# A two-block transformer step in one kernel: VectorE instead of GpSimd sums the rows of w_ada, one fused multiply-add per 128x1024 piece

## The chip, the core and the metric

One Trainium2 chip, of which the kernel uses one core. The metric is the time of the whole program on the device in microseconds, the median of several runs. The profile comes from one execution of its own, taken by the hardware profiler.

## What is computed

A batch of one sequence, 256 tokens of 2048 features in float32, goes through a first block and then a second one. Cut to what matters here:

```
c_act = silu(c)                                  # (1, 2048)
mod   = c_act @ w_ada + b_ada                    # w_ada: 2048 x 12288
sh1, sc1, gt1, sh2, sc2, gt2 = split(mod, 6)     # 6 pieces of 2048

h = rms_norm(x, g_mix) * (1 + sc1) + sh1
z = h @ w_in                                     # q, k, v (two attentions), indexer, gates
merged = sigmoid(gate_sb) * (stick_breaking(z) @ w_o_sb) + sigmoid(gate_ds) * (top64_attention(z) @ w_o_dsa)
x = x + gt1 * (merged @ w_out)

h = rms_norm(x, g_ffn) * (1 + sc2) + sh2
x = x + gt2 * ((silu(conv3(h @ w_gate)) * (h @ w_up)) @ w_down)
x = rms_norm(x, g_final)
# second block: gated linear attention, then a SwiGLU of the same width (5632)
```

The product `c_act @ w_ada` has a single row on the left. It isn't made by matmuls with w_ada as an operand: for each group of 128 rows of w_ada, all its rows are scaled by their entry of c_act, and the 16 groups are added up in one tile of 128 partitions; TensorE then adds the 128 partitions with a vector of ones.

## The kernel before, in words

**Matmuls.** Every large product is made in float32 accuracy from rounded parts. A weight slab of 128x2048 numbers (1 MB, four blocks of 128 rows by 512 columns) is fetched into `raw`, a ring of 4 slabs. A half is half a slab, 128x1024. ScalarE casts each half into `whi` (line 818), VectorE subtracts to get the remainder `wlo` (line 1206, "the split"), and TensorE makes 12 matmuls of 512 columns per half (lines 391 to 393). `whi` and `wlo` are rings of 4 halves, so a cast of half i waits until TensorE is through with half i-4, and at most three finished halves lie ahead of TensorE.

**Stages.** The list PHASES names them: A (48 halves, q, k, v of the first attention; an 80-column projection of the indexer lies between halves 15 and 16), B (64 halves, with the stick-breaking attention between them, one head per 8 halves), C1 (32, with the indexer's scores), C2 (32, it begins with a top-64 on VectorE and has the sparse attention between halves), O (32, output projections), U (32, w_out), F1p, F1 and F1e (16, 240 and 8 halves, the feed-forward), then the second block: GQ, GV, GR, GO, F2p, F2, F2e. With 24, 32, 16, 16, 16, 16 and 8 slabs, the stages A to F1p hold slabs 0 to 127. `body` on ScalarE and VectorE runs 4 halves ahead of its stage: its index idx goes from 4 to 19, and steps of attention, drains of PSUM and so on are hooks that run behind the split of a given idx. All engines work their programs in order.

**w_ada.** Pieces 0 and 1 (sh1, sc1) are summed at the very start by VectorE, in one `scalar_tensor_tensor` per 128x4096 rows (line 1273). The other four (4, 3, 2, 5 in that order: sc2, sh2, gt1, gt2) are summed by GpSimd in the background of A to F1: a chunk of 128x1024 (512 KB) comes into one of the two buffers of `ada_in`, GpSimd multiplies it by a column of c_act that it has copied into `acol` (line 1766), in place (line 1758), adds it to `ada_acc` (line 1760), and counts it in `ada_left`. There are 32 chunks per piece, 128 in all. When a piece is complete, TensorE adds the partitions: `ada_columns(0)` and `ada_columns(1)` (line 435, sc2 and sh2 as columns) behind A and behind C1, `ada_rows` (line 442) in U and in F1e. GpSimd clears `ada_acc` in between (line 1774). GpSimd also lays out the heads for the attentions (`sb_stage`, `ix_stage`, `qk_stage`, `v_stage`), between two pairs of chunks.

**The order of the fetches.** SyncE issues all DMAs, in program order. A slab waits until the slab four before it has been split (`lo_made`, line 233), a chunk until the chunk two before it has been added (`ada_left`, line 240). The chunks stand between slabs. Behind A, SyncE writes the table of distance biases to DRAM, waits for it, and loads 16 shifted copies of it into `hank0` and `hank1` (lines 285 to 293), which C2 uses.

Of the kernel before, what the change touches and what calls it, by code (L numbers as in the profile page):

```python
# [5 lines left out]
P = 128  # L6
S = 256
TB = S // P
D = 2048
KT = D // P  # L10
NB = 512
# [39 lines left out]


def build_program(nc, A, out):
# [28 lines left out]
    ada_in = at("ada_in", [P, 2, D // 2], ADA)  # L82
    ada_acc = at("ada_acc", [P, D], ADA + 8 * KB)
# [139 lines left out]
    ada_left = sem("ada_left")  # L223
# [5 lines left out]
    def _(sp):  # L229
        def slab(it, phase, per, s, src):  # L230

            if not (phase == "A" and s < RING and isinstance(it, int)):
# [3 lines left out]
        def ada_chunk(n, piece, j):  # L236

            if not (isinstance(n, int) and n < 2):
                sp.wait_ge(ada_left, n - 1)
            kt, half = (j // 2, j % 2) if isinstance(j, int) else j  # L240
# [26 lines left out]
        def a_body(it):  # L267
            for s in range(8):
                slab(it, "A", 16, s, w_in[:, 4 * (s % 4):4 * (s % 4) + 4, ds(it * 2 * NB + s // 4 * NB, NB)])
                ada_chunk(8 * it + s + 8, 4, ((8 * it + s + 8) // 2 if isinstance(it, int) else 4 * it + s // 2 + 4, s % 2))  # L270
        for s in range(RING):
            slab(0, "A", 16, s, w_in[:, 4 * s:4 * s + 4, 0:NB])
        for j in range(6):
            ada_chunk(j, 4, j)
        for s in range(RING, 8):
            slab(0, "A", 16, s, w_in[:, 4 * (s % 4):4 * (s % 4) + 4, NB:2 * NB])
            for j in range(2):
                ada_chunk(6 + 2 * (s - RING) + j, 4, 6 + 2 * (s - RING) + j)
        for j in range(14, 16):
            ada_chunk(j, 4, j)  # L280
        with sp.Fori(1, 3) as it:
            a_body(it)
# [3 lines left out]
        sp.wait_ge(sem("e_out"), 16)  # L286

        sp.wait_ge(sem("tt_T"), KT // 2)
        for h in range(NH):
            src = e_dram[h:h + 1, 0:P]  # L290
            sp.dma_start(hank1[:, h, :], bass.AP(tensor=src.tensor, offset=src.offset, ap=[[1, P], [1, S]])).then_inc(sem("hank_in"), 16)
            src = e_dram[h:h + 1, P:2 * P]
# [1711 lines left out]
```

## Time and profile before

| | |
|---|---|
| median of 3 runs | 3091.49 us (3090.83 to 3091.84) |
| profiled execution, first to last instruction (its span) | 3088.4 us |
| what lies around the span, against the median | 3.1 us |
| TensorE busy | 2772.0 us, 90% |
| VectorE busy | 2006.4 us, 65% |
| ScalarE busy | 1288.5 us, 42% |
| GpSimd busy | 1037.5 us, 34% |
| mean granted TensorE clock | 0.960 |
| moved by DMA | 585.40 MB, mean 190 GB/s |

The profiled execution has no time of its own beside its span. In the profile, PE is TensorE, PEld its weight load, DVE is VectorE, ACT ScalarE, POOL GpSimd, and SP SyncE. "Clock" is the share of the full clock that the throttle granted to TensorE; there are two levels, 0.5 and 1. A busy share is a mean over the span, and the stages of this kernel differ; so the rows below cut the span at the ends of the stages. "x" counts instructions that begin in a stretch. An L with a number is a line of the program before.

### The profile page before, as it was taken

The page shows a single profiled execution, that of the slowest core. Times are in us where ns is not written, and L with a number is a line of the kernel's source. Part 1 is how long each engine was busy: PE and PEld are TensorE (multiplying, and loading weights), DVE is VectorE, ACT ScalarE, POOL GpSimd, SP SyncE. Part 2 cuts the span into 40 slices and gives each one's busy share as a digit, 9 for nine tenths or more (in the row PEclk, how much of TensorE's full clock was granted, in tenths as well). Part 3 has the DMA queues.
Part 4 walks back from the last instruction along what each step waited for, and adds up shares of the span by engine and source line. Part 5 has one row for each costly group of instructions (what it writes and reads, how often), then busy time and mean ns, then how long its engine had stood idle before and what let it go on. Part 6 is the DMA issues. An engine that isn't in the chain of part 4 may idle for free. (4 is left out here: it accounts for less than half of the span.)

```text
span 3088.4 us, 35464 instructions
## 1 busy us (share of the span) xinstructions
PE 2772.0 (90%) x12279; PEld 2258.1 (73%) x12279; DVE 2006.4 (65%) x1808; ACT 1288.5 (42%) x1505; POOL 1037.5 (34%) x538
## 2 busy tenths in 40 slices
PE   0599899989988799999999959998898999999998
PEld 0477787667767678888788748777587888888886
DVE  7776566887975777677766674456655555555554
ACT  1223455334433444444444434444245444444443
POOL 0598454858945433222322250002200111111111
PEclk9989899989999899999999979998999999999999
DMA  9666554746664665655666515454054555555553
GB/s 392 240 205 230 198 206 175 245 144 210 242 234 164 236 204 190 204 195 191 198 204 207 187 55 187 153 177 150 1 164 152 190 190 190 190 191 190 189 190 122
DMA packets 266919, 585.40 MB, mean 190 GB/s; under 512 B 14300, under 2 KB 16676, under 8 KB 263900
## 3 DMA queue, kind: packets, MB, share of 16 engines
q1 hardware_dynamic: 266844, 584.41, 56.1%
q8 instruction: 45, 0.74, 0.1%
q14 instruction: 30, 0.25, 0.0%
HBM read 582.26 MB, written 2.11 MB: 189 GB/s over the span
## 5 line engine op out<-in xcount | busy, mean ns | idle before, releaser
L1206 DVE TENSOR_TENSOR sb_wlo<-sb_raw,sb_whi 128x1024 fp32r<-128x1024 f32 x896 | 1322.9, 1487 | 883.4 <-ACT sb_whi L818 882.5
L818 ACT ACTIVATE sb_whi<-sb_raw 128x1024 fp32r<-128x1024 f32 x896 | 945.2, 1059 | 1452.8 <-PE lin L393 1250.8
L391 PE MATMUL lin<-sb_whi,sb_act_hi 128*128 128x512 f32 x2880 | 1154.9, 401 | 89.7 <-DVE sb_wlo L1206 46.4
L393 PE MATMUL lin<-sb_whi,sb_act_lo 128*128 128x512 f32 x2880 | 1136.2, 395 | 0.0
L392 PE MATMUL lin<-sb_wlo,sb_act_hi 128*128 128x512 f32 x2880 | 1136.0, 394 | 0.0
L391 PEld LDWEIGHTS lin<-sb_whi,sb_act_hi 128*128 128x128 f32 x2880 | 550.7, 191 | 218.9 <-issue 53.2
L393 PEld LDWEIGHTS lin<-sb_whi,sb_act_lo 128*128 128x128 f32 x2880 | 549.6, 191 | 117.9
L392 PEld LDWEIGHTS lin<-sb_wlo,sb_act_hi 128*128 128x128 f32 x2880 | 551.3, 191 | 111.8 <-issue 0.2
L1758 POOL TENSOR_TENSOR sb_ada_in<-sb_ada_in,sb_small 128x1024 f32<-128x1024 f32 x128 | 301.0, 2351 | 293.5 <-DMA sb_ada_in<-in_w_ada_dram 174.7
L1760 POOL TENSOR_TENSOR sb_ada_acc<-sb_ada_acc,sb_ada_in 128x1024 f32<-128x1024 f32 x128 | 383.4, 2995 | 10.0
L391 PE MATMUL lin<-sb_whi,sb_hid_hi 128*128 128x512 f32 x704 | 278.4, 395 | 6.3 <-DVE sb_hid_lo L1487 3.7
L392 PE MATMUL lin<-sb_wlo,sb_hid_hi 128*128 128x512 f32 x704 | 275.5, 391 | 0.0
L393 PE MATMUL lin<-sb_whi,sb_hid_lo 128*128 128x512 f32 x704 | 275.5, 391 | 0.0
L1891 POOL TENSOR_TENSOR sb_x<-sb_x,sb_dstage 128x512 f32<-128x512 f32 x44 | 76.9, 1749 | 398.1 <-ACT sb_dstage L832 398.1
L1891 POOL TENSOR_TENSOR sb_yacc<-sb_yacc,sb_dstage 128x512 f32<-128x512 f32 x44 | 83.5, 1899 | 368.1 <-ACT sb_dstage L832 368.1
L391 PEld LDWEIGHTS lin<-sb_whi,sb_hid_hi 128*128 128x128 f32 x704 | 133.2, 189 | 37.6 <-DVE sb_hid_lo L1487 4.1
L393 PEld LDWEIGHTS lin<-sb_whi,sb_hid_lo 128*128 128x128 f32 x704 | 133.1, 189 | 28.1
L392 PEld LDWEIGHTS lin<-sb_wlo,sb_hid_hi 128*128 128x128 f32 x704 | 133.2, 189 | 27.3 <-issue 0.2
L1942 POOL TENSOR_TENSOR sb_ge<-sb_gb 128x256 f32<-128x256 f32 x24 | 17.5, 731 | 314.7 <-PE lin L393 282.9
L1897 POOL TENSOR_TENSOR sb_ubuf<-sb_ubuf,sb_cacc 128x512 f32<-128x512 f32 x11 | 19.5, 1773 | 257.5 <-ACT sb_ubuf L832 257.5
L453 PE MATMUL aux<-sb_onehot,sb_relb 32*8 32x512 f32 x2 | 1.9, 1036 | 87.8 <-DMA sb_relb<-in_rel_bias_dram 87.8
L1273 DVE SCALAR_TENSOR_TENSOR sb_acc<-sb_ada,sb_small,sb_acc 128x4096 f32<-128x4096 f32 x16 | 71.7, 4483 | 4.7 <-DMA sb_ada<-in_w_ada_dram 4.1
(292 smaller groups left out, 1770.5 us busy)
## 6 DMA issues: line engine op xcount, KB each, us to landing
sb_raw<-in_w_in_dram SPq DMA_DIRECT2D x88, 1024.0 KB, 5.9
sb_raw<-in_ffn_w_gu_dram SPq DMA_DIRECT2D x88, 1024.0 KB, 5.1
sb_ada_in<-in_w_ada_dram SPq DMA_DIRECT2D x128, 512.0 KB, 3.9
sb_raw<-in_gla_w_in_dram SPq DMA_DIRECT2D x48, 1024.0 KB, 5.2
sb_raw<-in_w_gate_dram SPq DMA_DIRECT2D x44, 1024.0 KB, 5.3
sb_raw<-in_w_up_dram SPq DMA_DIRECT2D x44, 1024.0 KB, 5.2
sb_raw<-in_w_down_dram SPq DMA_DIRECT2D x44, 1024.0 KB, 5.1
sb_raw<-in_ffn_w_down_dram SPq DMA_DIRECT2D x44, 1024.0 KB, 5.0
```

The source lines that it names most:

```text
L391: pe.matmul(o, x_hi[:, kt + q, t], whi[:, w], start=first and q == 0, stop=False)
L392: pe.matmul(o, x_hi[:, kt + q, t], wlo[:, w], start=False, stop=False)
L393: m = pe.matmul(o, x_lo[:, kt + q, t], whi[:, w], start=False, stop=last and q == 1)
L453: pe.matmul(aux[3][0:NH, :], relb[:], onehot[:], start=True, stop=True).then_inc(sem("erow_T"), 1)
L818: act.activation(whi[:, idx % RING * HALF:(idx % RING + 1) * HALF], raw[:, idx // 2 % RING, idx % 2 * HALF:(idx % 2 + 1) * HALF], ACT.Copy ...
L1206: dve.tensor_tensor(wlo[:, c], raw[:, idx // 2 % RING, idx % 2 * HALF:(idx % 2 + 1) * HALF], whi[:, c].bitcast(fp32), ALU.subtract).then_i ...
L1273: dve.scalar_tensor_tensor(acc0[:], ada0[:, u, :], cact[:, ds(4 * it + u, 1)], acc0[:], ALU.mult, ALU.add).then_inc(sem("ada0_sum"), 1)
L1758: pool.tensor_tensor(ada_in[:, half, :], ada_in[:, half, :], col.to_broadcast([P, D // 2]), ALU.mult).then_inc(sem("ada_mul"), 1)
L1760: pool.tensor_tensor(ada_acc[:, c], ada_acc[:, c], ada_in[:, half, :], ALU.add).then_inc(sem("ada_sum"), 1)
L1891: pool.tensor_tensor(y[:, 0, s], y[:, 0, s], dstage[:, c % 2, :], ALU.add).then_inc(sem("dstage_free"), 1)
L1897: pool.tensor_tensor(ubuf[:, 0, :], ubuf[:, 0, :], cacc[:].rearrange("p a t -> p (a t)")[:, 0:NB], ALU.mult).then_inc(sem("up_mul"), 1)
L1942: pool.tensor_tensor(e[:, :, 1, :], b[:, :, 1, :], ref, ALU.subtract)
```

## The change

VectorE takes over the 128 chunks. Each is one instruction: the chunk times an entry per partition of c_act, plus the sum so far. The first chunk of each half of a piece is a plain multiplication that overwrites, so nothing is cleared. The first piece has a tile of its own, `ada_first`, in the space of x, whose content is used up by then. GpSimd keeps only its other work, and its layouts no longer stand between pairs of chunks.

The chunks are dealt to slabs by a table, CHUNKS_AT: chunk n belongs to slab n+4 (n under 64), n+8 (under 96), n+20 (under 102); 102 and 103 belong to slabs 124 and 125, 104 and 105 to slab 126, 106 and 107 to slab 127. SyncE fetches the chunk right behind its slab, once the chunk two before it is added. VectorE adds it behind the split of the slab's second half and that half's hooks. In F1 the chunks keep their place in SyncE's order, and VectorE adds them at idx 21 and 23.

Three things move. The table loads go from behind A to behind the first slab of C1's second half. `ada_columns(0)` goes from behind A to behind B, and what VectorE makes of it (`mod_made`) with it; `ada_columns(1)` from behind C1 into C1, behind half 27. Loops of A, B, C1, C2 and O are written out where a chunk's number has to be a constant.

```
+ADA_PIECES = (4, 3, 2, 5)
+CHUNKS_AT = {}
+for _n in range(108):
+    _at = 4 + _n if _n < 64 else 8 + _n if _n < 96 else 20 + _n if _n < 102 else (124, 125, 126, 126, 127, 127)[_n - 102]
+    CHUNKS_AT.setdefault(_at, []).append(_n)
+def chunks_after(phase, it, per, s):
+    return CHUNKS_AT.get(H0[phase] // 2 + it * per // 2 + s, []) if isinstance(it, int) else []
...
+    ada_first = at("ada_first", [P, D], XB)
...
 SyncE
         def slab(it, phase, per, s, src):
...
             sp.dma_start(raw[:, s % RING, :].rearrange("p (k n) -> p k n", k=4), src).then_inc(slab_in[s % RING], 16)
+            for n in chunks_after(phase, it, per, s):
+                ada_chunk(n)
+        def ada_chunk(n, kt=None, half=None):
             if not (isinstance(n, int) and n < 2):
-                sp.wait_ge(ada_left, n - 1)
+                sp.wait_ge(sem("ada_sum"), n - 1)
...
+        for it in range(4):
+            cols_body(it, "B", 6 * NB)
+        def hankels():
+            sp.wait_ge(sem("e_out"), 16)
+            sp.wait_ge(sem("ada_T"), 1)
+            for h in range(NH):
...
+        for it in range(2):
+            cols_body(it, "C1", C_GATE, hankels if it else None)
...
 TensorE
         m.then_inc(sem("kix_T"), 1)
-        ada_columns(0)
...
-        pe.wait_ge(sem("mod_made"), 1)
...
         pe.wait_ge(sem("sb_out"), NH)
+        ada_columns(0)
...
+                if (it, idx) == (1, 11):
+                    pe.wait_ge(sem("mod_made"), 1)
+                    ada_columns(1)
...
 VectorE
+        def ada_add(n, kt=None, half=None):
+            first = isinstance(n, int) and n % 32 < 2
+            if kt is None:
+                kt, half = n % 32 // 2, n % 2
+            acc = ada_first if isinstance(n, int) and n < 32 else ada_acc
+            c = slice(half * (D // 2), (half + 1) * (D // 2))
+            dve.wait_ge(ada_come[half], 8 * (n - half) + 16)
+            if first:
+                if n >= 64:
+                    dve.wait_ge(sem("ada_T"), n // 32)
+                dve.tensor_scalar(acc[:, c], ada_in[:, half, :], cact[:, kt:kt + 1], None, ALU.mult).then_inc(sem("ada_sum"), 1)
+            else:
+                dve.wait_ge(sem("ada_sum"), n - 1)
+                dve.scalar_tensor_tensor(acc[:, c], ada_in[:, half, :], cact[:, ds(kt, 1)], acc[:, c], ALU.mult, ALU.add).then_inc(sem("ada_sum"), 1)
         def body(it, phase, per, hooks, upto=None, start=RING):
             for idx in range(start, per + RING if upto is None else upto):
                 split(it, phase, per, idx)
                 for step in hooks.get(idx, ()):
                     step()
+                if idx % 2:
+                    for n in chunks_after(phase, it, per, idx // 2):
+                        ada_add(n)
...
+                if n == 0 and phase == name:
+                    for half in range(2):
+                        add(21 + 2 * half, lambda half=half: ada_add(108 + 2 * it + half, 6 + it, half))
...
 GpSimd
-        def ada(n, kt, half, col):
-        def pairs_of(n, kt, count):
-        def clear(piece):
...
-        def b_pool(it, more):
+        with pool.Fori(0, 3) as it:
             for u in range(2):
-                kk = 2 * it + u
-                pairs_of(32 + 2 * kk, kk, 16 + kk)
-                if more:
-                    pool.wait_ge(sem("sb_o"), 2 * it + u + 1)
-                    sb_stage(2 * it + u + 2, u)
+                pool.wait_ge(sem("sb_o"), 2 * it + u + 1)
+                sb_stage(2 * it + u + 2, u)
```

## Rows read from the trace of the kernel before

**Rows 1.** The page, part 1: busy us, share of the span, instructions
```profile
PE 2772.0 (90%) x12279; PEld 2258.1 (73%) x12279; DVE 2006.4 (65%) x1808; ACT 1288.5 (42%) x1505; POOL 1037.5 (34%) x538
```

**Rows 2.** Stages; window, length, busy us per engine (instructions), clock, DMA share, GB/s
```profile
113.20:195.40 82.20, 58.45 (x226) 45.67 (x227) 76.61 (x34) 25.74 (x35) 77.68 (x36) 0.92 0.48 154
195.40:225.20 29.80, 29.80 (x146) 27.19 (x145) 17.41 (x8) 7.12 (x8) 27.34 (x14) 0.71 0.81 273
225.20:301.30 76.10, 76.10 (x336) 62.69 (x334) 56.01 (x28) 27.89 (x28) 71.05 (x29) 1.00 0.67 225
301.30:328.30 27.00, 7.36 (x36) 7.26 (x35) 7.54 (x11) 6.28 (x8) 2.98 (x4) 0.58 0.72 253
328.30:532.10 203.80, 199.90 (x909) 165.73 (x910) 126.77 (x126) 109.63 (x127) 98.68 (x47) 0.98 0.55 196
532.10:653.50 121.40, 106.30 (x472) 81.90 (x470) 102.57 (x69) 44.35 (x61) 93.93 (x52) 0.93 0.61 208
653.50:787.70 134.20, 120.47 (x566) 99.88 (x565) 103.89 (x145) 49.70 (x91) 102.91 (x56) 0.94 0.54 188
787.70:895.50 107.80, 93.39 (x388) 74.97 (x387) 104.78 (x58) 51.24 (x50) 92.49 (x37) 0.94 0.72 253
895.50:1011.30 115.80, 101.86 (x424) 82.07 (x424) 68.46 (x53) 38.16 (x42) 52.80 (x27) 0.93 0.51 175
1011.30:1081.00 69.70, 52.00 (x234) 43.15 (x234) 54.36 (x54) 36.46 (x47) 25.56 (x16) 0.88 0.66 228
...
1094.30:1767.60 673.30, 664.57 (x2984) 544.91 (x2983) 473.82 (x455) 307.98 (x337) 187.37 (x85) 1.00 0.61 199
2331.20:2389.00 57.80, 49.34 (x225) 41.25 (x226) 32.28 (x38) 32.73 (x43) 1.27 (x1) 0.91 0.44 145
```

**Rows 3.** The same for line 393 alone (4 matmuls per half), in B and C1
```profile
354.60:403.60 49.00, 25.00 (x64) 12.02 (x64) 1.00 0.59 210
...
641.30:653.50 12.20, 6.24 (x16) 3.00 (x16) 1.00 0.32 123
```

**Rows 4.** The page, part 5: GpSimd's multiplication and addition, busy us, mean ns
```profile
L1758 POOL TENSOR_TENSOR sb_ada_in<-sb_ada_in,sb_small 128x1024 f32<-128x1024 f32 x128 | 301.0, 2351 | 293.5 <-DMA sb_ada_in<-in_w_ada_dram 174.7
L1760 POOL TENSOR_TENSOR sb_ada_acc<-sb_ada_acc,sb_ada_in 128x1024 f32<-128x1024 f32 x128 | 383.4, 2995 | 10.0
```

**Rows 5.** SyncE's own waits; waiting line and releaser, total us, times, longest
```profile
SPq L241 <- POOLq L1762: 641.2, 98, 25.2
```

**Rows 6.** Line 1206 in A and in F2; count, ns minimum/median/maximum
```profile
L1206 DVE TENSOR_TENSOR sb_wlo<-sb_raw,sb_whi x48: 1210/2372/3418, 113.8 to 293.9; 128x1024 fp32r<-128x1024 f32 x48
...
L1206 DVE TENSOR_TENSOR sb_wlo<-sb_raw,sb_whi x240: 1224/1225/1227, 2390.2 to 3049.3; 128x1024 fp32r<-128x1024 f32 x120
```

**Rows 7.** Line 1206 alone by stage, A, C2 and O: length, VectorE busy us
```profile
113.80:301.30 187.50, 110.94 (x48) 0.92 0.61 202
...
653.50:787.70 134.20, 64.17 (x32) 0.94 0.54 188
787.70:895.50 107.80, 74.68 (x33) 0.94 0.72 253
```

**Rows 8.** The page, part 5: the fused operation at 128x4096
```profile
L1273 DVE SCALAR_TENSOR_TENSOR sb_acc<-sb_ada,sb_small,sb_acc 128x4096 f32<-128x4096 f32 x16 | 71.7, 4483 | 4.7 <-DMA sb_ada<-in_w_ada_dram 4.1
```

**Rows 9.** The page, part 6: slabs of w_in, KB each, median us to landing
```profile
sb_raw<-in_w_in_dram SPq DMA_DIRECT2D x88, 1024.0 KB, 5.9
```

**Rows 10.** Timeline of TensorE, the start of F2p: start, us, idle before
```profile
2339.66 3.67 PE L421 MATMUL aux<-sb_con,sb_xs 128*128 128x128 f32 x16 [8.50 <-ACT sb_xs L855]
```

**Rows 11.** Timeline of SyncE behind A: issues
```profile
289.86 0.33 SPq L241 DMA_DIRECT2D sb_ada_in<-in_w_ada_dram  x1
...
301.48 0.39 SPq L234 DMA_DIRECT2D sb_raw<-in_w_in_dram  x1
```

**Rows 12.** Timeline of VectorE in B: first hook of a head, next splits
```profile
366.69 0.54 DVE L1324 TENSOR_SCALAR sb_lb<-aux 128x384 f32<-128x384 f32 x1
...
371.91 3.49 DVE L1206 TENSOR_TENSOR sb_wlo<-sb_raw,sb_whi 128x1024 fp32r<-128x1024 f32 x3
```

More of the change, by code:

```diff
@@ L265, in _, with cols_body @@
         sp.dma_start(relb[:], A["rel_bias"]).then_inc(sem("rel_in"), 16)
-        def a_body(it):
+        def cols_body(it, phase, col0, after=None):
             for s in range(8):
[L269 to L282, printed above, removed]
+                slab(it, phase, 16, s, w_in[:, 4 * (s % 4):4 * (s % 4) + 4, it * 2 * NB + col0 + s // 4 * NB:it * 2 * NB + col0 + s // 4 * NB + NB])
@@ L284, in _ @@
+                if after and s == 0:
+                    after()
+        for it in range(3):
+            cols_body(it, "A", 0)
         sp.wait_ge(sem("erow_held"), 1)
         sp.dma_start(e_dram, erow[:]).then_inc(sem("e_out"), 16)
[L286 to L292, printed above, removed]
-            sp.dma_start(hank0[:, h, :], bass.AP(tensor=src.tensor, offset=src.offset, ap=[[1, P], [1, P]])).then_inc(sem("hank_in"), 16)
@@ L314, in _ @@
+        for it in range(2):
+            cols_body(it, "C1", C_GATE, hankels if it else None)
+        for it in range(2):
+            cols_body(it, "C2", C_GATE + D)
+        for it in range(2):
+            for s in range(8):
+                c = it * 2 * NB + s // 4 * NB
+                slab(it, "O", 16, s, w_o[s % 4 // 2][:, 4 * (s % 2):4 * (s % 2) + 4, c:c + NB])
         sp.wait_ge(half_used, H0["O"])
@@ L1300, in _ @@
         body(0, "A", 16, drains2(0, "A", lambda k: sbz[:, 1, k * NB:(k + 1) * NB], {9: [split_ix]}), start=8)
-        with dve.Fori(1, 3) as it:
+        for it in range(1, 3):
             body(it, "A", 16, drains2(it, "A", lambda k: sbz[:, 1, cols(it, k)]))
@@ L1361, in ix_dve @@
             return {4 * u + 6: [lambda u=u: add(u)] for u in range(4)}
-        with dve.Fori(0, 2) as it:
+        for it in range(2):
             body(it, "C1", 16, drains2(it, "C1", lambda k: gate_sb[:, 1, cols(it, k)], ix_dve(it)))
@@ L1405, in ds_dve @@
             return hooks
-        with dve.Fori(0, 2) as it:
+        for it in range(2):
             body(it, "C2", 16, drains2(it, "C2", lambda k: gate_ds[:, 1, cols(it, k)], ds_dve(it)))
@@ L1428, in o_hooks @@
             return {4 * gi + 7: [lambda gi=gi: take(gi)] for gi in range(4)}
-        with dve.Fori(0, 2) as it:
+        for it in range(2):
             body(it, "O", 16, o_hooks(it))
@@ L1813, in _ @@
         ix_stage(1, 1)
[L1815 to L1826 removed]
+        for p in range(2, NIX // 2):
+            pool.wait_ge(sem("ix_T"), p - 1)
+            ix_stage(p, p)
         def qk_stage(h, u):
```

121 lines of the change are left out of this document (26 added, 95 removed).

## The prediction

> **What bounds the kernel now.** The first thing to read is the share of each engine over the whole span [rows 1]: TensorE 90%, VectorE 65%, GpSimd 34%. Taken alone it says "TensorE-bound", and that would leave this change nothing to win. So the next view is the busy time by stage [rows 2], cut where TensorE ends the last matmul of a stage. From 1094 us on TensorE is busy for 664.6 of 673.3 us, and behind that come stages that the change doesn't touch. From 113 to 1094 us it isn't: TensorE works 7.4 of the 27 us behind A, and idles 10 to 25% of C1, C2, O, U and F1p, at a granted clock of 0.88 to 0.94 (1.00, that is 2.4 GHz, in the end of A, where it never pauses).
>
> The yardstick is a stretch in which TensorE never waits. A half (one 128x1024 piece, 12 matmuls) takes 76.1/28 = 2.72 us in the end of A [rows 2], 49.0/16 = 3.06 us in B, where attention matmuls lie between, and 12.2/4 = 3.05 us in the end of C1 [rows 3]. A slab (1 MB, two halves) therefore takes 5.44 us at the least.
>
> Against that stand three costs of GpSimd's sum. First, its own pace: a piece takes 2.35 + 3.00 us [rows 4], with the waits between and a column copy for every second one about 6.0 (an estimate: GpSimd is busy 71 of 76 us in the end of A for some 12 pieces, [rows 2]), over the 5.44 us of a slab. Second, the order on SyncE: the fetch of the next piece waits for GpSimd, 641 us in total over 98 waits, and the next slab stands behind it [rows 5]. Third, VectorE: a split lasts 1.225 us without variation where GpSimd is quiet, and 1.21 to 3.42 us in A [rows 6]. 3.42 is 1.2 plus about one GpSimd instruction. Times the counts: A's 48 splits take 110.9 us instead of 58.8, C2's 32 take 64.2 instead of 39.2, O's 33 take 74.7 instead of 40.4 [rows 7].
>
> The Trainium skill says the same in SBUF — State Buffer, "Who interferes with whom": a VectorE instruction with two SBUF inputs and a GpSimd instruction that reads SBUF exclude each other, and the later one is blocked until the other ends. By that rule the trace agrees (1.21 against 3.42 us). The same skill has a rule that speaks against this change, in Perfetto Trace Analysis, "Optimizing Scalar/DVE Operations": with a saturated VectorE, handing work to ScalarE or even GpSimd may pay; it adds that between VectorE and GpSimd this may fail because of the shared port. Followed to its end it gives the second rival below.
>
> **What the change adds.** 108 pieces outside F1's loop and 20 in it move to VectorE, one instruction each. The trace has the same operation at 128x4096: 4483 ns [rows 8], a quarter of which is 1.12 us; the split, also two SBUF inputs of 1024, takes 1.225 [rows 6]. I take 1.23; 1.12 and, if something else still holds it up, 1.6 are the ends. In all 128 x 1.23 = 157 us of VectorE, against 301 + 383 = 684 us of GpSimd removed [rows 4]. Per slab of A that is 2 x 1.225 + 1.23 = 3.7 us plus 0.3 for a drain, under 5.44: hidden. On SyncE a piece now waits until the piece two before it is added, that is until VectorE is past slab s-2, so slab s+1 starts three slabs ahead and no longer four. That leaves about 5 halves x 2.72 minus 3.5 us (cast, split, add) = 10 us for a landing of 5.9 us [rows 9]: hidden too, with 4 us to spare.
>
> **Stage by stage, all against the profiled execution** (span 3088.4 us; the timed runs have a median of 3091.5, 3.1 us around the span):
> - Head of A. TensorE starts at 113.2 and is through 16 halves at 195.4. The same work stands undisturbed in F2p: first transposes at 2339.7, 16 halves done at 2389.0, 49.3 us [rows 10]. A must split four halves first, 3.4 us more. So 53 instead of 82: -29. The other 105.9 us of A (the 80-column projection at a clock of 0.71, then full pace) stay.
> - A to B. The 27.0 us before B and the first half-clock halves go. SyncE issued a piece at 289.9 and the next slab only at 301.5 [rows 11]; between them stand 16 loads of the distance table and one round trip, and these move into C1. The 32 column sums, nearly all of the 7.4 us that TensorE works there [rows 2], move behind B. What stays: split 19, drain, one add of 1.23 ahead of kdup, two copies, transposes, a cast: about 6.3 us, 0.7 of transposes and 3 at the lower clock. B's 64 halves at 3.06 are 196.2. 206.2 against 230.8: -25. B is the tightest: per 8 halves VectorE has 8 x 1.225 + 4 x 1.23 + about 7.9 us (the 5.2 us from 366.7 to 371.9 of a head's first hook, 1.7 of its second, a drain; [rows 12]) = 22.6 of 24.5 us.
> - C1. 32 halves at 3.12 us (12.2 per four where no drain falls in [rows 3], 12.5 taken) = 99.8, column sums twice (3.7 each at full clock, an estimate: half of 6.8 us at the lower one, and a little), 1.2 of start, 2 at the lower clock, 1.5 for the 16 table loads that now lie in SyncE's queue ahead of a slab (7.5 us of issue, 4 of them covered by the lead in fetches, the rest by 6 us of prepared halves). 112 against 121.4: -9. Bounds of the table loads: 0 and 6.
> - C2. It begins with 15 us of top-k on VectorE, which stays and gets one add ahead of it. After that splits save 64.2 - 39.2 = 25 us and 16 adds put back 20. TensorE idles 13.7 us here [rows 2], most of it in the top-k and where a head's softmax meets splits, and both stay: -2, from -7 to +8.
> - O. Per four halves 4.9 + 2.5 + 2.0 = 9.4 of 10.9 us: full pace, 7 x 10.9 = 76.2, and 20 for the first four, with a wait of 6 us for the splits of attention's output. 96.4 against 107.8: -11.
> - U. TensorE idles 13.9 of 115.8 us [rows 2], 5 of them at the start; the other 9, and 4 for halves at the lower clock after them, are slabs that stood on SyncE behind a piece waiting for GpSimd; the row sum and the start stay: -13.
> - F1p. 57.8 us of F2p [rows 2] is the undisturbed case, plus 2 for a table load and gate transposes: 60 against 69.7: -10.
> - Into F1: pieces 104 to 107 come two at a time behind slabs 126 and 127, and behind them on SyncE the four loads of biases and gains, then F1's first slab. That slab is now asked for once half 9 of F1p is split, then only behind the add at half 13: 4 x 2.72 = 11 us later, with 6 to 9 us of cover (the lead in fetches and three prepared halves): +4, from 0 to 10.
> - F1 and what follows: two adds at idx 21 and 23, where VectorE idles 1.5 us per half; the stage is at TensorE's pace: 0, from -9 (its small waits go) to +5.
>
> Sum: -29 - 25 - 9 - 2 - 11 - 13 - 10 + 4 = -95. 3091.5 - 95 = 2996 us (span 2993).
>
> **The rivals.**
> 1. VectorE becomes the bound (the rule on saturated engines, as a mechanism here). In B it has 1.9 us to spare per head, and its hooks wait in order for ScalarE's exponentials. One add falls between the two hooks of a head and delays the second by 1.2 us. If an add costs 1.6 us or a cast comes late, each of 8 heads loses 2 us, C1 wins 3 instead of 9, C2 loses 8 instead of winning 2: +16, +6 and +10, so 3028. For it: 92% load. Against it: TensorE has up to three prepared halves, 9 us, to live on, and a head's burst, 5.2 + 1.2 + 1.7 us, is shorter.
> 2. Slabs come late, because each stands behind an add. If landing with a piece in front is 1 to 2 us longer than the spare, 104 slabs lose 0.6 us each: +62, so 3058. Against it: the end of A already fetches nearly the same bytes per slab at 225 GB/s with the engines of the queues busy 0.67 of the time [rows 2].
> 3. Slower than before: the same loop, binding hard. Three slabs may be under way per landing L plus 4.7 us of cast, splits and add, so a slab costs (L + 4.7)/3. It binds from L = 11.6 us. To eat all that is won from 225 us to 1011 us, each of the 110 slabs there would have to cost what it does now, 786/110 = 7.1, and with the 29 us of A's head 7.4: L = 17.5 us, against a median of 5.9 [rows 9]. Were L 19, a slab would cost 7.9 and the time would be about 3091.5 + 0.5 x 110 = 3146.
> 4. More is given back than I count: C2 keeps all 7, F1's waits go, nothing is lost into F1: 2996 - 5 - 9 - 4 = 2978.
>
> **How the numbers follow.** Forecast 0.58, 2996, with its own range 2975 to 3015; rival 1 0.20, rival 2 0.07, rival 3 0.03, rival 4 0.10, and 0.02 for no change, by two of them together. The range reaches up to rival 1 with its upper terms and down below rival 4: 2962 to 3045. Faster by over 0.2% 0.95, within 0.2% 0.02, slower by over 0.2% 0.03; 0.2%, 6 us, is about what a measurement of this kernel can tell from no change.
>
> **What would show each step.** Splits at 1.225 us nearly all through; about 50 us for the first 16 halves; under 12 us between A's last matmul and B's first; 12.2 us per four halves in B; no ScalarE cast waiting for a slab DMA in U; the stretch behind 1094 us as long as now. The forecast is wrong if TensorE waits for the weights in B (rival 1), if casts wait for slab DMAs in every stage (rivals 2 and 3), or if the new instruction takes much over 1.25 us.

## The result

| | before | changed |
|---|---|---|
| median | 3091.4 us (4 runs) | 2989.2 us (4 runs, 2983.2 to 2992.8) |
| profiled execution, span | 3088.4 us | 2990.8 us (its own time 2992.77 us) |
| ratio of the times | | 0.967, 95% interval 0.9657 to 0.9684 |

The change is 102 us faster, 3.3%. Forecast were 2996 us, from 2962 to 3045. Between the two profiled spans lie 97.6 us; all shares below are parts of these. First the page of the changed kernel, part 1 (as [rows 1]): busy us, share of the span, instructions.

```profile
PE 2749.4 (92%) x12279; PEld 2248.6 (75%) x12279; DVE 1850.3 (62%) x1936; ACT 1291.7 (43%) x1505; POOL 303.6 (10%) x214
```

VectorE has 128 instructions more than before and 156 us less busy time, though the adds are in it (128 x 1.28 = 164 us, by the row below). So its other instructions got 320 us shorter together: what GpSimd's work had put on them [rows 6]. The next line is of the changed kernel's page, part 5: the fused add. Below it stands the split (before L1206, now L1205) in A alone (count, ns minimum/median/maximum).

```profile
L1222 DVE SCALAR_TENSOR_TENSOR sb_ada_acc<-sb_ada_in,sb_small,sb_ada_acc 128x1024 f32<-128x1024 f32 x90 | 114.9, 1279 | 0.0
```

```profile
L1205 DVE TENSOR_TENSOR sb_wlo<-sb_raw,sb_whi x51: 1217/1226/1228, 113.1 to 270.7; 128x1024 fp32r<-128x1024 f32 x51
```

In A the split has no variation left (before 1210 to 3418 ns). The add takes 1.28 us; 1.23 was forecast. Now the stages of the changed kernel, cut as [rows 2] at TensorE's last matmul of each: window, length, busy us of PE, PEld, DVE, ACT and POOL, clock, DMA share, GB/s. In order they are the head of A (16 halves), the rest of A, A's end to B's end, C1, C2, O, U, F1p, the first four halves of F1, and the rest of F1.

```profile
112.52:166.37 53.85, 50.94 (x227) 42.27 (x227) 38.21 (x42) 28.46 (x37) 0.00 (x0) 0.97 0.57 198
166.37:272.30 105.93, 105.91 (x480) 89.91 (x479) 60.45 (x52) 35.94 (x36) 0.00 (x0) 0.92 0.69 238
272.30:477.00 204.70, 198.14 (x911) 164.76 (x912) 150.17 (x164) 112.35 (x132) 7.46 (x8) 0.98 0.70 245
477.00:590.10 113.10, 112.28 (x532) 89.61 (x531) 69.00 (x84) 44.28 (x61) 12.15 (x12) 0.94 0.66 226
590.10:713.20 123.10, 112.74 (x534) 93.99 (x534) 91.61 (x161) 50.61 (x91) 6.26 (x12) 0.96 0.58 203
713.20:808.40 95.20, 90.28 (x389) 74.12 (x387) 71.44 (x71) 50.03 (x50) 0.00 (x0) 0.96 0.76 270
808.40:911.00 102.60, 96.67 (x424) 78.94 (x424) 64.29 (x61) 40.58 (x45) 9.88 (x6) 0.97 0.61 211
911.00:971.40 60.40, 50.49 (x233) 41.82 (x232) 42.32 (x50) 30.81 (x41) 4.67 (x3) 0.92 0.52 173
971.40:992.20 20.80, 14.65 (x58) 11.95 (x58) 14.03 (x18) 10.96 (x11) 0.00 (x0) 0.84 1.03 383
992.20:1665.30 673.10, 664.22 (x2984) 545.43 (x2983) 446.50 (x473) 307.94 (x334) 75.86 (x40) 1.00 0.60 198
```

Against [rows 2], in us:

| stage | before | changed | difference | forecast |
|---|---|---|---|---|
| A, to its end | 188.1 | 159.8 | -28.3 | -29 |
| A's end to B's end | 230.8 | 204.7 | -26.1 | -25 |
| C1 | 121.4 | 113.1 | -8.3 | -9 |
| C2 | 134.2 | 123.1 | -11.1 | -2 |
| O | 107.8 | 95.2 | -12.6 | -11 |
| U | 115.8 | 102.6 | -13.2 | -13 |
| F1p | 69.7 | 60.4 | -9.3 | -10 |
| first four halves of F1 | 13.3 | 20.8 | +7.5 | +4 |
| rest of F1 | 673.3 | 673.1 | -0.2 | 0 |
| behind F1 | | | +4.6 | 0 |

(0.7 us are missing in the table: TensorE starts A that much earlier. "Behind F1" reaches to the end of the span.) Most of the gain came where it was forecast. Three lines are off: C2 won five times as much, F1 begins later than expected, and 4.6 us are lost behind F1, where no instruction was changed.

### The profile page after: what moved, and what is told of

It is laid out like the page before. It is cut to its first block and busy times, and to the rows that moved or that the text cites. A ratio compares the mean times of both kernels' runs of the same rounds, so it can differ in the third digit from the quotient of the medians.

```text
span 2990.8 us, 34105 instructions
## 1 busy us (share of the span) xinstructions
PE 2749.4 (92%) x12279; PEld 2248.6 (75%) x12279; DVE 1850.3 (62%) x1936; ACT 1291.7 (43%) x1505; POOL 303.6 (10%) x214
## 5 line engine op out<-in xcount | busy, mean ns | idle before, releaser
L1205 DVE TENSOR_TENSOR sb_wlo<-sb_raw,sb_whi 128x1024 fp32r<-128x1024 f32 x896 | 1106.4, 1237 | 940.3 <-ACT sb_whi L817 940.0
L388 PEld LDWEIGHTS lin<-sb_whi,sb_act_hi 128*128 128x128 f32 x2880 | 548.1, 190 | 164.6 <-DVE sb_wlo L1205 25.2
L389 PEld LDWEIGHTS lin<-sb_wlo,sb_act_hi 128*128 128x128 f32 x2880 | 548.2, 190 | 110.9 <-issue 0.2
L1222 DVE SCALAR_TENSOR_TENSOR sb_ada_acc<-sb_ada_in,sb_small,sb_ada_acc 128x1024 f32<-128x1024 f32 x90 | 114.9, 1279 | 0.0
L1524 DVE SCALAR_TENSOR_TENSOR sb_cacc<-sb_gpad,sb_par,sb_cacc 128x256 f32<-128x256 f32 x88 | 58.5, 706 | 6.1 <-DVE sb_cacc L1524 1.6
L418 PE MATMUL aux<-sb_con,sb_xs 128*128 128x128 f32 x96 | 17.7, 342 | 44.1 <-issue 35.6
```

What stands on the lines that cost most here:

```text
L388: pe.matmul(o, x_hi[:, kt + q, t], whi[:, w], start=first and q == 0, stop=False)
L389: pe.matmul(o, x_hi[:, kt + q, t], wlo[:, w], start=False, stop=False)
L418: m = pe.transpose(aux[n % 4][:, q * S + tb * P:q * S + (tb + 1) * P], src[:, tb, (2 * g + q) * P:(2 * g + q + 1) * P], ident)
L1205: dve.tensor_tensor(wlo[:, c], raw[:, idx // 2 % RING, idx % 2 * HALF:(idx % 2 + 1) * HALF], whi[:, c].bitcast(fp32), ALU.subtract).then_i ...
L1222: dve.scalar_tensor_tensor(acc[:, c], ada_in[:, half, :], cact[:, ds(kt, 1)], acc[:, c], ALU.mult, ALU.add).then_inc(sem("ada_sum"), 1)
L1524: m = dve.scalar_tensor_tensor(cacc[:, f, :], gpad[:, f, 2 - k:2 - k + S], col(w, f), cacc[:, f, :], ALU.mult, ALU.add)
```

## The experiments

The forecast gave two reasons for what GpSimd costs: its reads hold up VectorE, and its pace and the order on SyncE hold up the slabs. The change removes both at once, and it moves the table loads and the column sums besides, so its result can't tell them apart. The first three runs part the two costs of GpSimd; no run parts the moves from them. Two more measure how much room VectorE has left, and the others test the three lines that are off.

### GpSimd keeps its pace but no longer reads

```
-            pool.tensor_tensor(ada_in[:, half, :], ada_in[:, half, :], col.to_broadcast([P, D // 2]), ALU.mult).then_inc(sem("ada_mul"), 1)
+            for r in range(2):
+                link(pool.memset(ada_in[:, half, :], 0.0))
+            pool.memset(ada_in[:, half, 0:D // 4], 0.0).then_inc(sem("ada_mul"), 1)
...
-            pool.tensor_tensor(ada_acc[:, c], ada_acc[:, c], ada_in[:, half, :], ALU.add).then_inc(sem("ada_sum"), 1)
+            for r in range(2):
+                link(pool.memset(ada_acc[:, c], 0.0))
+            pool.memset(ada_acc[:, c], 0.0).then_inc(sem("ada_sum"), 1)
```

(Shortened: in the kernel before, for the first 108 chunks, with GpSimd's loops of A and B written out and its column copy a memset too. The sums of these chunks are left out.)

> The kernel before, with GpSimd's multiplication and addition of the first 108 chunks replaced by memsets (two and a half, and three, of 128x1024, about 2.3 and 2.8 us), and its column copy by a memset. The sums of these chunks are left out; GpSimd's pace, the order on SyncE and the waits on both stay, but GpSimd reads nothing in SBUF during them. It parts the two costs of GpSimd's sum. Theory, that both count: splits last 1.22 us in every stage; A's head is about 29 us shorter, O about 10, C2 and F1p together 5; the stretch A to B and U stay as they are, since SyncE still waits behind GpSimd; together -45 us against the kernel before (-35 to -55). Rival, pace and order alone: splits are short but the stages as long as before, within 10 us of it. Rival, port alone: the whole gain of 95 to 100 us comes.

Measured: 3037.9 us (3035.7 to 3041.8), ratio to before 0.983 (0.9814 to 0.9847), so -52 us. Its line 1206 in A, what ScalarE waits for in A, and SyncE's waits for GpSimd over the whole span (us in total, times, longest):

```profile
L1206 DVE TENSOR_TENSOR sb_wlo<-sb_raw,sb_whi x48: 1216/1220/1228, 113.5 to 287.7; 128x1024 fp32r<-128x1024 f32 x48
```

```profile
ACT sb_whi L818 <- DMA sb_raw<-in_w_in_dram: 102.4, 19, 21.1
```

```profile
SPq L241 <- POOLq L1772: 617.0, 100, 24.5
```

Its stages, A to F1p:

```profile
113.50:293.70 180.20, 161.90 (x703) 132.55 (x701) 71.28 (x70) 58.40 (x69) 164.56 (x199) 0.93 0.62 207
293.70:519.80 226.10, 204.29 (x943) 171.40 (x944) 118.83 (x137) 116.22 (x135) 96.12 (x116) 0.94 0.59 209
519.80:622.20 102.40, 98.89 (x471) 77.77 (x470) 50.66 (x65) 43.00 (x61) 90.19 (x116) 1.00 0.68 235
622.20:748.60 126.40, 116.83 (x566) 97.31 (x565) 76.64 (x148) 49.44 (x92) 96.29 (x121) 0.96 0.58 200
748.60:843.40 94.80, 90.64 (x389) 74.41 (x387) 55.04 (x57) 50.07 (x50) 83.37 (x101) 0.96 0.80 284
843.40:960.70 117.30, 101.24 (x425) 81.37 (x424) 57.07 (x55) 39.16 (x44) 53.43 (x58) 0.93 0.53 184
960.70:1024.20 63.50, 50.26 (x234) 41.97 (x234) 43.22 (x53) 36.65 (x47) 30.62 (x33) 0.89 0.72 254
```

GpSimd is nearly as busy as before (614.6 against 645.4 us from A to F1p) and SyncE waits for it nearly as long (617 against 641 us), yet every split in A is at 1.22 us. So it is GpSimd's reading that holds up VectorE. The Trainium skill says just this in SBUF — State Buffer, "Who interferes with whom": two SBUF inputs on VectorE contend with a GpSimd instruction that reads SBUF, not with one that only writes it; by that rule this trace agrees.

The total is as forecast, but not its split by stage. O (-13.0) wins all that the change wins there, C2 (-7.8) and F1p (-6.2) two thirds of it, and C1, which the expectation doesn't name, wins 19.0. (The change's C1 has column sums in it. Without them it would be at about 99.4 us, an estimate from the run with spread sums below, 107.2 less 7.8; so 19.0 are most of 22.) Contention was most of what these four paid. U wins nothing. A, for which 29 us were forecast, wins 7.9 (180.2 against 188.1), and the 20 us left to the changed kernel's A are slabs: ScalarE now waits 102.4 us for w_in in A, before 24.6 (a view of its waits in the same stretch). Two limits of nearly the same pace lay behind each other in A. The one that the trace of before showed, a slow VectorE, hid the second; taking it away alone brings little.

### GpSimd's reads put back beside the change

```
+        def load(count):
+            for _ in range(count):
+                n = done[0]
+                if n >= 4:
+                    pool.wait_ge(sem("ada_sum"), n - 3)
+                for _ in range(7):
+                    link(pool.tensor_tensor(scratch[:], con[:, 0:256], con[:, 256:512], ALU.mult))
+                done[0] += 1
```

(Called for 108 chunks, in B twice ahead of each `sb_stage` and twice behind it.)

> The changed kernel, and beside it GpSimd makes seven tensor_tensor of 128x256 (about 0.73 us each) on scratch memory for each chunk, started by VectorE's count of the chunks; nobody waits for them. So the order and pace of the change with the contention brought back, in short instructions. Theory, that a VectorE instruction with two SBUF inputs waits for the GpSimd instruction under way: splits last 1.22 to about 2.0 us, mean 1.5 to 1.7 where GpSimd works, and no longer up to 3.4; TensorE takes 2.72 us per half and VectorE's split and half an add then take about 2.5, so most of it stays hidden: +5 to +25 us against the changed kernel, in A's head, B and C2. Rival, that contention depends on the bytes GpSimd moves and not on the length of one instruction: mean split above 2 us and +40 us or more. Rival, no contention from such small operations: splits at 1.22 to 1.3 us and no change in time.

Measured: 3090.6 us (3086.0 to 3093.2), ratio to before 0.9999: the whole gain is gone, +101 us against the changed kernel, far outside the expected +5 to +25. Its split in A and GpSimd's operation in A (ns minimum/median/maximum), then B by window:

```profile
L1206 DVE TENSOR_TENSOR sb_wlo<-sb_raw,sb_whi x51: 1212/1737/1780, 113.0 to 273.5; 128x1024 fp32r<-128x1024 f32 x51
```

```profile
L1783 POOL TENSOR_TENSOR sb_scratch<-sb_con x101: 724/1597/1794, 112.6 to 274.2; 128x256 f32<-128x256 f32 x101
```

```profile
274.40:532.80 258.40, 211.81 (x911) 171.12 (x910) 185.82 (x162) 111.09 (x130) 232.83 (x204) 0.91 0.56 192
```

The durations are as the theory has them. A split grows by 0.5 us, no more than one short GpSimd instruction (0.72 us undisturbed), and GpSimd's grows from 0.72 to about 1.6, by less than one split: each waits for the other. But A's end comes only 2 us later (274.4) and O is 4 us longer (99.4), while B is 54 us longer, and C1 and C2 together 36 (272.0 against 236.2). In B TensorE waits for this (timeline of TensorE, one of four such gaps; idle before it in brackets):

```profile
440.21 1.12 PE L494 MATMUL aux<-sb_con,sb_st_sb 128*128 128x128 f32 x4 [7.87 <-POOL sb_st_sb L1792]
```

It waits for GpSimd's layout of a head, which stands behind up to four loads of 7 x 1.16 us on GpSimd's own queue. TensorE's waits for such layouts are 28.7 us in B and 24.3 in C1 and C2 (views of its waits); in the kernel before and in the changed one there are none. So this run mixed contention with a second cause of my own making, and its 101 us are no price of contention.

> The run with GpSimd's reads beside the sums again, with three instead of seven operations of 128x256 per chunk, and with GpSimd's layouts of heads put ahead of them in its order. The run before it cost 101 us; its TensorE waits in B are for GpSimd's layouts, which stood behind up to four loads of 8 us. Theory, that splits of 1.75 us cost little by themselves (A +2, O +4 in that run, where nobody waits for GpSimd) and that the rest came from work queued on GpSimd: splits still reach 1.75 us, B is within 8 us of the changed kernel's 204.7 us, and the time is +5 to +20 us against the changed kernel. Rival, contention itself costs: B +20 us or more and the time +40 us or more.

The edit: `range(7)` becomes `range(3)`, and each layout comes ahead of the loads. Measured: 3000.3 us (2999.0 to 3002.5), ratio to before 0.9709 (0.9694 to 0.9724); +11 us against the changed kernel. Its split in B, and the stretch of B:

```profile
L1206 DVE TENSOR_TENSOR sb_wlo<-sb_raw,sb_whi x63: 1210/1635/1847, 273.4 to 481.0; 128x1024 fp32r<-128x1024 f32 x63
```

```profile
272.30:482.70 210.40, 201.32 (x910) 164.81 (x910) 168.35 (x160) 110.44 (x130) 131.10 (x104) 0.98 0.67 235
```

The splits are almost as long as in the run before, and B costs 5.7 us instead of 54. The theory holds in its first half: with splits of 1.64 us on the median TensorE nearly stays fed. TensorE no longer waits for a layout in B, so what hurt was a queue on which attention waited. Whether the order or the smaller load cured it is open, since the run changes both. In the kernel before the layouts also stand between pairs of chunks, but no TensorE wait for them is in its trace.

### How much room VectorE has

```
-                dve.scalar_tensor_tensor(acc[:, c], ada_in[:, half, :], cact[:, ds(kt, 1)], acc[:, c], ALU.mult, ALU.add).then_inc(sem("ada_sum"), 1)
+                o = slice(c.start, c.start + 1)
+                dve.scalar_tensor_tensor(acc[:, o], ada_in[:, half, 0:1], cact[:, ds(kt, 1)], acc[:, o], ALU.mult, ALU.add).then_inc(sem("ada_sum"), 1)
```

> The changed kernel, except that each fused add outside the first of a half works on one column of the chunk instead of 1024; so the sums of w_ada are left out, while the instruction, its waits and every fetch stay. 120 of 128 adds shrink from 1.28 us to about 0.1. My theory, that the adds lie beside TensorE's work: only the add ahead of kdup between A and B, and those in front of a stage's first splits, are on the path, so -1 to -5 us against the changed kernel (2984 to 2988), B and C2 as long as they are (204.7 and 123.1 us). Rival, that VectorE is near its bound: C2 and B are shorter by 3 us or more each, and the time is 2980 or less.

Measured: 2983.5 us (2980.4 to 2984.9), -5.7 against the changed kernel's median, a little more than the expected -1 to -5 (-4.1 against its later median, at the end of this section). Its stages B and C2:

```profile
272.80:477.20 204.40, 198.72 (x912) 165.15 (x912) 120.67 (x164) 113.27 (x132) 6.56 (x8) 0.98 0.71 245
...
587.20:710.50 123.30, 113.16 (x533) 94.34 (x534) 75.71 (x161) 50.59 (x91) 6.17 (x12) 0.96 0.60 206
```

Without the adds VectorE is 29.5 us less busy in B and 15.9 in C2, and neither stage is shorter (204.4 and 123.3). The adds lie beside TensorE's work. (C1 took 110.0 us, 3 less; it takes 108.5 in the repeated run of the changed kernel below, so this can't be put down to the edit.)

The other way, each add cut in two operations:

```
+                dve.tensor_tensor(ada_in[:, half, :], ada_in[:, half, :], cact[:, ds(kt, 1)].to_broadcast([P, D // 2]), ALU.mult).then_inc(sem("ada_mul"), 1)
+                dve.wait_ge(sem("ada_mul"), n - 1 - 2 * (n // 32) if isinstance(n, int) else n - 7)
+                dve.tensor_tensor(acc[:, c], acc[:, c], ada_in[:, half, :], ALU.add).then_inc(sem("ada_sum"), 1)
```

> The changed kernel with the fused add cut in two: VectorE multiplies the chunk in place, waits for that, and adds it, about 2.5 us instead of 1.28 for each of 120 chunks. VectorE's busy time in B goes from 150 to about 188 us of 204.7, in C2 from 92 to about 111 of 123, in O from 71 to about 92 of 95. Theory: at a load of 92 to 97% the prepared halves no longer carry a head's burst everywhere; B +5, C2 +5, the other stages +1 each, so +15 us (2 to 30) against the changed kernel. Rival 1 of the prediction, in which an add of 1.6 us already costs 2 us per head: +40 us or more. The other rival, slack everywhere: within 3 us, which would say that the fusion is worth nothing.

Measured: 3012.7 us (3010.2 to 3016.6), ratio to before 0.9742, so +23.5 us against the changed kernel. The two operations take 1.22 and 1.33 us. Its B and C2, and TensorE's waits in B (us in total, times, longest):

```profile
272.20:492.70 220.50, 202.88 (x910) 164.25 (x910) 181.52 (x191) 109.72 (x131) 9.99 (x8) 0.98 0.65 224
607.10:730.20 123.10, 112.74 (x534) 93.98 (x534) 108.49 (x176) 49.90 (x91) 9.27 (x12) 0.96 0.58 200
```

```profile
...
PE aux L512 <- DVE sb_lb L1354: 5.3, 7, 0.8
PE aux L505 <- DVE sb_lk L1347: 4.7, 6, 0.9
```

The total is in the range, the places aren't: B pays 16 us instead of 5 (and the wait at F1's start grows by 3.4 us, to 9.5), C2 nothing, though VectorE is 88% busy there. And in B, at 82%, TensorE doesn't wait for splits but for VectorE's steps of attention (`lb`, `lk`), 10 us in 13 waits. A busy share doesn't say where an engine becomes late; a hook does on which TensorE waits with nothing prepared. This is the first rival's mechanism. It costs its 2 us per head at 2.5 us per add, and nothing at the 1.28 us that the fused add takes. So the fusion is worth about 23 us, mostly in B.

### The wait at the start of F1

```
-    _at = 4 + _n if _n < 64 else 8 + _n if _n < 96 else 20 + _n if _n < 102 else (124, 125, 126, 126, 127, 127)[_n - 102]
+    _at = 4 + _n if _n < 64 else 8 + _n if _n < 96 else 16 + _n if _n < 106 else 18 + _n
```

In the changed kernel (timelines of SyncE, TensorE and ScalarE around F1's start; start, us, idle before in brackets) SyncE asks for chunks 106 and 107, then for four loads of biases and gains, and only then, at 962.23, for F1's first slab:

```profile
957.84 1.53 SPq L256 DMA_DIRECT2D sb_ada_in<-in_w_ada_dram  x2
...
962.23 10.11 SPq L245 DMA_DIRECT2D sb_raw<-in_w_gate_dram  x4
```

```profile
977.57 0.79 PE L388 MATMUL lin<-sb_whi,sb_act_hi 128*128 128x512 f32 x1 [6.15 <-DVE sb_wlo L1205]
```

```profile
975.20 2.00 ACT L817 ACTIVATE sb_whi<-sb_raw 128x1024 fp32r<-128x1024 f32 x2 [12.04 <-DMA sb_raw<-in_w_gate_dram]
```

> The changed kernel with another table for the last chunks outside F1: chunk n from 96 to 105 belongs to slab n+16, 106 and 107 to slabs 124 and 125, so that no slab carries two chunks and slabs 126 and 127 carry none. Theory: F1's first slab is then asked for as early as any other, TensorE's wait of 6.2 us at F1's start goes, and U and F1p stay as long as they are: -6 us against the changed kernel (-8 to -3). Rival, the wait comes from the four loads of biases and gains and their memory traffic, not from the doubled chunks: less than 2 us are won. Rival, four more chunks in U and at F1p's start delay slabs there: 0.

Measured: 2978.4 us (2974.9 to 2979.6), ratio to before 0.9639 (0.9624 to 0.9653), -10.8 against the changed kernel. The start of F1, and the whole of F1, in this run:

```profile
967.00:980.00 13.00, 13.00 (x63) 10.85 (x62) 9.02 (x10) 7.47 (x8) 0.00 (x0) 1.00 0.71 239
967.00:1652.00 685.00, 676.20 (x3041) 555.35 (x3039) 454.55 (x481) 314.29 (x341) 75.69 (x40) 1.00 0.60 198
```

TensorE never pauses into F1, and F1 takes 685.0 us instead of 693.9. Of the 8.9 us, 6.15 are the wait, and the other 2.7 about what the lower clock behind it costs, which the forecast of this run had left out (the changed kernel's first four halves run at a clock of 0.84). The four loads of biases are still there, ahead of the same slab; so it was the chunks on slabs 126 and 127 (the run undoubles them and moves them away at once). That is settled; that the median moved by 2 us more is within what the last run shows.

### Column sums spread over C1

```
-            for j in range(KT):
+            for j in range(4 * quarter, 4 * quarter + 4):
                 m = pe.matmul(aux[3][:, j:j + 1], acc[:, j * P:(j + 1) * P], ones[:, 0:1], start=True, stop=True)
...
+                if it == 0 and idx < 4:
+                    ada_columns(0, idx)
+                if it == 1 and 8 <= idx < 12:
```

> The changed kernel with each run of 16 column sums cut in four, 4 behind each of four halves of C1 (halves 0 to 3 for sc2, 24 to 27 for sh2), and VectorE's step on the first moved to its idx 9 in C1. In the changed kernel a run of 16 costs 6.8 to 8.5 us in C1, at the lower clock for 7 us. Theory, that the lower clock comes with 16 single-column sums in a row: at full clock they cost 3.7 us by the prediction's estimate, so C1 is 5 to 8 us shorter (105 to 108 instead of 113.1) and the time -6. Rival, a column sum costs its 0.43 us wherever it stands: C1 as long as it is, within 2 us. Rival, the four pieces each take the clock down: C1 longer by 5 us or more.

Measured: 2985.5 us (2982.6 to 2988.7), ratio to before 0.9657 (0.9642 to 0.9672); -3.7 against the changed kernel's first median, -2.2 against the later one below, and the ranges overlap. Of the 6 us that were expected, 3.7 at best. C1 of the changed kernel in three parts (the first four halves, sixteen halves in its middle, the last four), then its first run of column sums (busy us, mean ns; the second takes 4.6 us), then C1 of this experiment:

```profile
509.98:558.89 48.91, 48.91 (x234) 38.56 (x233) 35.49 (x42) 21.88 (x30) 9.28 (x8) 1.00 0.86 294
477.00:497.80 20.80, 19.98 (x95) 16.36 (x95) 11.01 (x15) 6.05 (x10) 2.07 (x3) 0.84 0.55 186
571.10:590.10 19.00, 19.00 (x91) 15.47 (x89) 6.95 (x10) 5.29 (x7) 0.00 (x0) 0.82 0.13 43
```

```profile
L433 PE MATMUL aux<-sb_con,sb_ada_first 128*128 128x1 f32 x32 | 4.5, 274 | 0.8 <-ACT sb_oT_sb L935 0.8
```

```profile
477.80:585.00 107.20, 106.31 (x532) 84.48 (x531) 68.94 (x84) 44.25 (x61) 11.70 (x12) 1.00 0.70 239
```

The middle runs at 12.2 us per four halves. Against that, the fours with the sums take 8.6 and 6.8 us more: 4.5 us of sums, and behind them a stretch at the lower clock, 0.84 and 0.82 on the mean, although TensorE never idles in the last four. Spread, the sums take 3.9 us a run and the clock stays at 1.00 all through C1. So the theory names the cause rightly, as far as these traces go: the clock falls behind sixteen single-column sums in a row, and not behind four. The price is smaller than 6 us, because the same program sometimes pays less for it, as the next run shows.

### The changed kernel once more, and both edits together

> The changed kernel once more, unchanged, to see how much of its time is a draw. In all profiles so far the stages behind F1 have the same instructions and gaps, and the time from F1's end to the program's last matmul is either 1315.7 or 1320.3 us: the long one where the granted clock falls 3.6 to 3.8 us after F1's last matmul, the short one where it falls 2.4 to 2.6 us after it. [...] Theory: the draw is new in every execution, so the times spread over 2983 to 2993 again, and if this profile falls on the short side, the stages behind F1 take 1315.7 us; the 5 us that the changed kernel's profile lost there are no part of the change. Rival, the 5 us belong to the changed program: its profile shows 1320.3 again, and 2988 to 2993 in nearly all runs.

Measured: 2987.7 us (2986.8 to 2987.8, 5 runs). C1 of this execution, and the stretch from F1's last matmul to the program's last one; below, the same stretch of the first profile of the changed kernel, and of the kernel before.

```profile
477.20:585.70 108.50, 107.67 (x533) 85.77 (x531) 68.99 (x84) 44.28 (x61) 12.00 (x12) 0.98 0.69 236
...
1663.20:2980.30 1317.10, 1234.41 (x5448) 999.45 (x5448) 722.71 (x735) 569.57 (x659) 185.85 (x128) 0.96 0.48 158
```

```profile
1665.30:2985.50 1320.20, 1236.58 (x5448) 1001.41 (x5448) 722.92 (x735) 569.69 (x659) 185.82 (x128) 0.96 0.48 158
```

```profile
1767.50:3083.20 1315.70, 1233.35 (x5449) 998.61 (x5448) 722.42 (x735) 569.53 (x659) 185.87 (x128) 0.96 0.49 158
```

The same program takes 1317.1 us here and 1320.2 there, and C1 108.5 and 113.1, with the same instructions. So these 3 to 5 us differ between executions of one program and belong to no kernel. The expectation was too simple in two points: 1317.1 is a third value, and these five runs don't spread over 10 us. What goes with the draw is when the clock falls behind F1's last matmul: after 2.5 us in the kernel before (1315.7 us), after 3.8 in the first profile of the changed kernel (1320.2). It isn't so that later means longer: in this last profile it falls after 4.0 us, with 1317.1. Below are windows of the first two; the clock is the third number from the end.

```profile
1767.50:1770.00 2.50, 0.05 (x1) 0.00 (x0) 1.32 (x2) 1.54 (x2) 0.00 (x0) 0.99 0.66 256
1770.00:1780.20 10.20, 5.87 (x17) 4.71 (x18) 3.01 (x4) 1.06 (x1) 0.00 (x0) 0.50 0.33 103
```

```profile
1665.30:1669.10 3.80, 0.77 (x7) 0.80 (x8) 1.83 (x2) 1.54 (x2) 0.00 (x0) 1.00 0.52 168
1669.10:1679.30 10.20, 6.47 (x17) 4.82 (x16) 2.52 (x3) 1.46 (x2) 0.00 (x0) 0.50 0.28 102
```

No run here shows what sets that instant. The Trainium skill says in TensorE: Matmul & The Clock Gate, Part 1, that the window in which TensorE's activity is judged runs free and isn't reset when a kernel starts; no run here shows that either, but it would give such a draw.

> Both of the last two edits together, the table without doubled chunks and the column sums spread over C1. Theory: the two lie in different stages and add up: -12 us against the changed kernel (-15 to -6), 2977. Rival: what is won ahead of the second block is given back later by longer stretches at the lower clock, as 5 us of the change's gain were: -6 or less in time although C1 and F1's start win 12.

Measured: 2974.7 us (2973.0 to 2975.9, 5 runs), ratio to before 0.9625 (0.9612 to 0.9638). That is the fastest kernel of this study, -14.5 us against the changed kernel's first median, -13.0 against its second, and -3.7 against the early pieces alone. In its profile C1 takes 107.2 us and F1 685.0, so both edits keep what they win alone, and behind F1 nothing is given back (about 1315.8 us from F1's end to the last matmul).

## Why the prediction was right, and where it wasn't

- **Head of A, -29.** Right in size (53.9 us for 16 halves, 53 forecast), half right in its reason. The prediction put it down to VectorE's 110.9 us of splits. With these gone alone, A wins 7.9; the rest is the pace of the slabs behind GpSimd's chunks, which the prediction had listed among its costs but not charged to A.
- **A to B, and B, -25.** -26.1. TensorE waits 5.7 us for `kdup` between the stages (6.3 worked out), and B runs at its 3.06 us per half. With GpSimd's reads alone gone this stretch wins 4.7. The rest is not GpSimd's pace alone: as the prediction says, the change moves the table loads and the column sums out of this gap. Before, TensorE did 6.8 us of sums there and waited 18.4 us for `kdup` (two lines of TensorE between 301 and 328.3 us below), and SyncE spent 11 us on the table, from 290.4 to the slab at 301.5 [rows 11]. So up to 18 of the 26 us (an estimate: 6.8 + 11) come from these two moves. That rival is untested: no run moves them and leaves the sum on GpSimd.

```profile
L435 PE MATMUL aux<-sb_con,sb_ada_acc 128*128 128x1 f32 x32 | 6.8, 348 | 0.0
...
L487 PE MATMUL aux<-sb_con,sb_kdup 128*128 128x128 f32 x2 | 0.7, 448 | 18.4 <-DVE sb_kdup L1308 18.4
```

- **C1, -9.** -8.3, by errors that cancel. Halves at 3.06 instead of 3.12 (-2.0) and no loss by the table loads (-1.5) against column sums of 4.5 us instead of 3.7 (+1.7) with more lower clock behind them, in this execution.
- **C2, -2.** -11.1, below the end of its range. The step that failed: 20 us of adds were set against 25 us of shorter splits, as if time on VectorE were time on the path. Adds off leaves C2 at 123.3, and two operations per chunk leave it at 123.1. What TensorE had waited for was VectorE's `qk_ds`, late behind long splits: 11.9 us in four waits before (the first line below, TensorE's waits in C2), 6.2 in one now. The prediction had said that these waits stay. The other 5.4 us are 1.1 of waits for softmax's `lg` that are gone too, and about 3 of lower clock (an estimate: a mean of 0.94 over 134.2 us before, 0.96 over 123.1 now); some 1 us stays unexplained.

```profile
PE aux L573 <- DVE sb_qk_ds L1383: 11.9, 4, 6.3
```

```profile
PE aux L572 <- DVE sb_qk_ds L1400: 6.2, 1, 6.2
```

One thing at C2's start bears on C1. There TensorE waits for VectorE's step on the column sums, which stands behind a split and a drain. Before, the second run of sums stood in this gap, 3.6 us with 0.7 us of waiting behind it. Now TensorE waits 4.2 us there (first line below, TensorE's waits in C2; the second is the run of sums before), and the sums make four halves of C1 6.8 us longer. So this move wins nothing at C2 and costs in C1. No run puts them back.

```profile
PE lin L388 <- DVEq L1384: 4.2, 1, 4.2
```

```profile
L435 PE MATMUL aux<-sb_con,sb_ada_acc 128*128 128x1 f32 x32 | 3.6, 247 | 0.0
```

- **O, U, F1p, -34 together.** -35.1. In O and F1p it was contention mainly (-13.0 and -6.2 of it without the order). U is the other kind: with GpSimd's pace kept, U is as long as before (117.3 us), so its 13 us are GpSimd's pace with the order on SyncE, as forecast.
- **Into F1, +4.** +7.5. The mechanism was right and named in advance. The term was mis-sized. The lateness was taken as 11 us; SyncE asks for the slab 9.2 us ahead of F1p's end (962.23 against 971.4), and with the early pieces 25.5 us ahead (941.52 against 967.0), so it is 16. Its cast begins 13.0 us after it was asked for, where the prediction counted a landing of 5.9. And the wait of 6.15 us is followed by halves at the lower clock, which were not priced.
- **F1, and behind it, 0.** F1 -0.2; behind it +4.6, which goes with the instant at which the clock falls; the repeated run has 3.1 us of it less, so it is no effect of the change.
- **The first rival** needs an add of more than 1.28 us. At 2.5 us it is there, in B alone, at its forecast 2 us per head. Its C2 and C1 terms didn't come. (The prediction says that the rule on saturated engines gives the second rival; it is this first one.)
- **Slabs behind adds** (second and third rival): a slab of w_in lands in 6.2 us on the median (the page, part 6), and the bound was 11.6. ScalarE still waits for a slab here and there (10.6 us in three waits for w_in, 6.9 in one for w_out, 4.8 in one for w_up), but only F1's first slab kept TensorE waiting.

The sum was -95 and the spans differ by 97.6: C2 won 9 more than forecast, and F1's start (3.5) and the draw (4.6) took most of that away again. So part of the closeness is luck. The median lies 7 us under the forecast and not 2: the profiled execution is the slowest of the first four, and its own time is 2.0 us over its span where 3.1 were assumed. Two terms are slightly off in their own working (64 x 3.06 is 195.8 and not 196.2, 76.2 + 20 is 96.2 and not 96.4), which changes nothing.

## What to carry to other kernels

An engine's busy time counts only where somebody waits for its result with nothing prepared: look for that wait first, then ask whether the added work stands ahead of it. When a trace shows one limit, estimate the second one behind it before you credit the whole stretch to the first; here a run that took contention alone away won 8 of A's 28 us. Extra work of TensorE is cheapest where it waits anyway (the second column sums stood so before; putting them back wasn't tried). Leave no two extra transfers ahead of the first slab of a stage, and keep layouts on which attention waits ahead of background work on the same queue.

## What the runs showed of the hardware

- VectorE's subtraction of two 128x1024 SBUF inputs takes 1.22 us beside GpSimd memsets that keep that engine over 90% busy (164.6 of 180.2 us), about 1.74 us beside its 128x256 reads, and up to 3.42 us beside its 128x1024 reads [rows 6]. What it pays each time is up to about one GpSimd instruction (0.5 us of 0.72, 2.2 of 2.35 to 3.0), so shorter instructions on GpSimd cost VectorE less each.
- It works both ways: GpSimd's 128x256 multiplication went from 0.72 to 1.6 us on the median, by less than one split.
- Thirty-two one-column matmuls in a row take 4.5 us and are followed by a stretch at the lower clock, without any pause of TensorE. Eight at a time between full matmuls leave the clock at 1.00 (3.9 us for 32).
- The same program took 1317.1 and 1320.2 us for one stretch and 108.5 and 113.1 us for another, with the clock falling at other instants. A difference of that size between two profiles of this kernel needs several profiles, or a view of the clock.
